# A six-mixer network on one core: the first loads in another order, two weight tiles split singly, half of x turned between products

## What is computed

```python
def short_conv_mixer(xn, w_in, conv_w, conv_b, w_out):
    bg, cg, hv, z = jnp.split(xn @ w_in, 4, axis=-1)
    u = cg * hv
    y = lax.conv_general_dilated(
        u, conv_w[:, None, :].astype(u.dtype), window_strides=(1,),
        padding=[(CONV_WIDTH - 1, 0)], dimension_numbers=("NWC", "WIO", "NWC"),
        feature_group_count=A_WIDTH) + conv_b
    return (bg * y * jax.nn.silu(z)) @ w_out
...
            y = short_conv_mixer(rmsnorm(x, a_norm[j]), a_w_in[j], a_conv_w[j], a_conv_b[j], a_w_out[j])
...
        x = x + y
```

## Time and profile before

| | us |
|---|---|
| timed runs | 931.11, 932.44, 932.61; median 932.44 |
| span of the profiled execution, first to last instruction | 928.8 |
| TensorE busy in it | 905.7 |
| VectorE, ScalarE, GpSimd busy | 649.8, 499.6, 299.3 |

### The profile page before, as it was taken

The page is one execution under the profiler, slowest core; times in us unless marked ns, Lnnn a source line. Parts: engine busy times, 40 slices in busy tenths (PEclk is TensorE's granted clock), DMA queues, the critical chain, the costliest instruction groups (busy, mean ns, idle before and its releaser), DMA issues.

```text
span 928.8 us, 16916 instructions
## 1 busy us (share of the span) xinstructions
PE 905.7 (98%) x6817; PEld 853.2 (92%) x6817; DVE 649.8 (70%) x1024; ACT 499.6 (54%) x732; POOL 299.3 (32%) x243
## 2 busy tenths in 40 slices
PE   8999999999989999989999999999999999999996
PEld 8999997788879987779999999999999998989996
DVE  5786666889785789865876676897735745656643
ACT  5644445664875669865444453343536336585632
POOL 8433322473111332113433218976003000223310
PEclk9999999999999999999999999999999999999998
DMA  9886436344414443445785535544664552525411
GB/s 247 234 224 181 181 106 240 121 140 169 147 60 150 143 134 112 145 117 153 183 225 187 182 137 182 178 146 178 236 217 164 209 182 91 181 92 181 165 41 46
DMA packets 123587, 148.72 MB, mean 160 GB/s; under 512 B 9562, under 2 KB 79103, under 8 KB 123519
## 3 DMA queue, kind: packets, MB, share of 16 engines
q1 hardware_dynamic: 121472, 145.63, 48.6%
q0 software_dynamic: 464, 1.02, 0.4%
q10 hardware_dynamic: 1582, 1.12, 0.4%
HBM read 146.70 MB, written 1.05 MB: 159 GB/s over the span
## 4 chain that ended last, share of the span: by engine, by line
PE 66%; DVE 9%; ACT 4%; POOL 1%; issue 1%; ACTq 0%; POOLq 0%; DVEq 0%
PE acc L1772 48%; PE aux L1772 17%; DVE wlo L931 2%; DVE wlo L952 1%; ACT work L705 1%; POOL sqy L1686 1%; ACT work L707 1%; DVE work L1270 1%; ACT work L720 1%; PE aux L2144 1%; DVE arena L1039 0%; DVE sqy L1130 0%; DVE hf L1140 0%; ACT arena L748 0%; ACT whi L491 0%
## 5 line engine op out<-in xcount | busy, mean ns | idle before, releaser
L931 DVE TENSOR_TENSOR wlo<-raw,whi 128x2048 fp32r<-128x2048 f32 (+5 forms) x114 | 273.5, 2421 | 81.7 <-ACT whi L483 79.7
L1772 PE MATMUL acc<-xh,whi 128*128 128x256 f32 x1128 | 321.7, 285 | 1.1 <-ACT arena L748 0.6
L1772 PE MATMUL acc<-xh,wlo 128*128 128x256 f32 x1128 | 319.1, 283 | 0.0
L1772 PE MATMUL acc<-xl,whi 128*128 128x256 f32 x1128 | 319.1, 283 | 0.0
L483 ACT ACTIVATE whi<-raw 128x2048 fp32r<-128x2048 f32 (+5 forms) x115 | 197.9, 1745 | 88.5 <-PE acc L1772 51.4
L1772 PEld LDWEIGHTS acc<-xh,whi 128*128 128x128 f32 x1128 | 215.9, 191 | 3.0 <-issue 1.6
L1772 PEld LDWEIGHTS acc<-xl,whi 128*128 128x128 f32 x1128 | 216.0, 191 | 0.0
L1772 PEld LDWEIGHTS acc<-xh,wlo 128*128 128x128 f32 x1128 | 215.9, 191 | 0.0
L1772 PE MATMUL aux<-yh,whi 128*128 128x256 f32 x288 | 82.3, 286 | 2.0 <-DVE stat L1274 2.0
L1772 PE MATMUL acc<-whi,xh 128*128 128x512 f32 (+1 forms) x208 | 81.4, 391 | 1.6 <-DVE arena L1039 0.5
L1772 PE MATMUL aux<-yl,whi 128*128 128x256 f32 x288 | 81.5, 283 | 0.0
(11 more groups left out here) (348 smaller groups left out, 1726.7 us busy)
## 6 DMA issues: line engine op xcount, KB each, us to landing
raw<-in_a_w_in SPq DMA_DIRECT2D x52, 512.0 KB, 6.7
raw<-in_sb_w_in SPq DMA_DIRECT2D x48, 512.0 KB, 5.5
raw<-in_b_w_in SPq DMA_DIRECT2D x36, 512.0 KB, 5.4
raw<-in_pool_w_in SPq DMA_DIRECT2D x32, 512.0 KB, 5.4
raw<-in_a_w_out SPq DMA_DIRECT2D x16, 512.0 KB, 4.9
raw<-in_pool_w_out SPq DMA_DIRECT2D x16, 512.0 KB, 5.7
raw<-in_sb_w_out SPq DMA_DIRECT2D x16, 512.0 KB, 5.2
raw<-in_b_w_out SPq DMA_DIRECT2D x8, 512.0 KB, 5.0
```

Of the source, the lines that this page charges most:

```text
L931: TT(wlo[b][:, lo:hi], (raw_third if third else raw[b])[:, lo:hi], whi[b][:, lo:hi].bitcast(F32), ALU.subtract).then_inc(lo_ready, 1)
L1772: return nc.tensor.matmul(out_, lhsT, rhs, start=start, stop=stop, skip_group_check=True)
```

## The change

The four issues of x on SP are taken apart: x's first half goes ahead of everything, the identity and the gain `a_norm` (from ScalarE's list) follow, then x's second half and the 48 rotary constants. The ten small rows move from ScalarE's list to SP's, behind the weight tiles of unit 0 and ahead of the other constants and unit 1's tiles. ScalarE's first instructions are now the two weight tiles, which get a semaphore each, and a load of its function table. GpSimd's four gain rows and mask move from ahead of the angles to behind them. Weight tiles 0 and 1 are split singly (`first_tile`), the other three quarters as before. TensorE does 14 and 5 idle products in place of 22 and 6, turns the first half of x, and turns the second half ahead of `k` 2 of unit 0 (`turn_x(1)`). VectorE and ScalarE have lists to match.

```diff
+            x_half(0)
+            sp.dma_start(ident, a["constants"][:, C_ID:C_ID + P]).then_inc(sem("ident_in"), 16)
+            sp.wait_ge(sem("grow_clear"), 1)
+            for dst, part in small_inputs(True):
+                sp.dma_start(dst, part).then_inc(sem("a_norm_in"), 16)
+            x_half(1)
+            sp.dma_start(cst[:, C_IROW:C_COLS], a["constants"][:, C_IROW:C_COLS]).then_inc(sem("inv_in"), 16)
...
                     for k in range(2, 8):
                         first_tile(0, k).then_inc(sem(f"first_in{k // 2}"), 16)
+                    for dst, part in small_inputs(False):
+                        sp.dma_start(dst, part).then_inc(sem("grow_in"), 16)
                     sp.dma_start(cst[:, P:C_IROW], a["constants"][:, P:C_IROW]).then_inc(sem("cst_in"), 16)
...
-                    .then_inc(sem("first_in0"), 16)
-            small_inputs(False)
+                    .then_inc(sem(f"tile_in{k}"), 16)
+            nc.scalar.preload_act_table_set("exp_and_others")
+
+            def first_tile(k):
+
+                c = slice(512 * k, 512 * k + 512)
+                act.wait_ge(sem(f"tile_in{k}"), 16)
+                A(whi[0][:, c], raw[0][:, c], ACT.Copy).then_inc(sem("first_hi") if k else sem("tile_hi"), 1)
...
                     for n in range(NK):
+                        if m == 0 and n in (0, 2):
+                            first_tile(n // 2)
+                        if m == 0 and n in (4, 5, 7):
+                            first_quarter(0, n - 3 if n < 7 else 3)
                         act.wait_ge(sem("x_ready"), 4 * m + n // 2 + 1)
                         A(xh[:, n, :], xT[:, n, :], ACT.Copy, scale=G[:, gain + n:gain + n + 1])\
                             .then_inc(sem("xh_ready"), 1)
-                        if m == 0 and n % 2:
-                            first_quarter(0, n // 2)
...
+                turned(0)
+                first_tile(0)
+                turned(1)
+                low(0)
+                first_tile(1)
+                low(1)
+                first_quarter(0, 1)
+                turned(2)
+                turned(3)
+                first_quarter(0, 2)
+                low(2)
+                low(3)
+                first_quarter(0, 3)
...
-                    if u < 2 and k % 4 == 0:
+                    if u == 0 and k == 0:
+                        pe.wait_ge(sem("tile_lo"), 1)
+                    if u < 2 and k % 4 == (1 if u == 0 and k < 4 else 0):
                         pe.wait_ge(sem("first_lo"), 2 * u + k // 4 + 1)
...
                 def before(k):
+                    if k == 2 and m == 0:
+                        turn_x(1)
                     pe.wait_ge(sem("xl_ready"), 8 * m + k + 1)
...
-            busy(22)
+            busy(14)
...
+            turn_x(0)
+            busy(5)
```

More of the change, by code:

```diff
@@ L335, in free_slot, with small_inputs @@
             eng.wait_ge(lo_ready, 2 * u - 2)
+        def small_inputs(first):
+            rows = ((G_A, "a_norm", 16), (G_CW, "a_conv_w", 48), (G_CB, "a_conv_b", 16), (G_B, "b_norm", 8),
+                    (G_C, "c_norm", 8), (G_N2, "norm_g_2", 16),
+                    (G_QL, "c_q_lat_norm", 3), (G_KVL, "c_kv_lat_norm", 2))
+            found = [(grow[col:col + c, 0, :], a[name].rearrange("(n c) -> n c", c=P))
+                     for col, name, c in (rows[:1] if first else rows[1:])]
+            if first:
+                return found
+            return found + [(grow[G_CQ:G_CQ + 1, 0, 0:64], a["c_q_norm"][:, 0:64]),
+                            (grow[0:1, 1, 0:64], a["c_k_norm"][:, 0:64]),
+                            (grow[1:17, 1, :], a["pool_scale_2"].rearrange("(n c) -> n c", c=P))]
         @block.sync
@@ L400, in conv_layer, with x_half @@
                     plain(u0 + 8 + h, a["a_w_out"][j], 4 * h, 0)
-            sp.dma_start(ident, a["constants"][:, C_ID:C_ID + P]).then_inc(sem("ident_in"), 16)
-            sp.dma_start(cst[:, C_IROW:C_COLS], a["constants"][:, C_IROW:C_COLS]).then_inc(sem("inv_in"), 16)
-            for half in range(2):
+            def x_half(half):
                 c = slice(512 * half, 512 * half + 512)
@@ L966, in split, with first_tile, first_x, turned @@
                     split_half(u % 2, cut, end)
+            def first_tile(k):
+                c = slice(512 * k, 512 * k + 512)
+                dve.wait_ge(sem("first_hi") if k else sem("tile_hi"), 1)
+                TT(wlo[0][:, c], raw[0][:, c], whi[0][:, c].bitcast(F32), ALU.subtract)\
+                    .then_inc(sem("first_lo") if k else sem("tile_lo"), 1)
+            def first_x():
+                def turned(c):
+                    dve.wait_ge(sem("x_psum"), c + 1)
+                    V.tensor_copy(xT[:, 2 * c:2 * c + 2, :], aux[:, c, :].rearrange("p (n t) -> p n t", n=2))\
+                        .then_inc(sem("x_ready"), 1)
+                def low(c):
+                    dve.wait_ge(sem("x_ready"), c + 1)
+                    for n in (2 * c, 2 * c + 1):
+                        dve.wait_ge(sem("xh_ready"), n + 1)
+                        STT(xl[:, n, :], xT[:, n, :], G[:, G_A + n:G_A + n + 1], xh[:, n, :].bitcast(F32),
+                            ALU.mult, ALU.subtract).then_inc(sem("xl_ready"), 1)
+                turned(0)
[11 more added lines that the diff above has]
+                first_quarter(0, 3)
             def renorm(m, gain):
@@ L1640, in by_token @@
                 return ap.rearrange("p (t c) -> p t c", t=1).broadcast_to([P, NT, ap.shape[1]])
+            for n, name in enumerate(("b_q_norm", "b_k_norm")):
+                pool.dma_start(gain_b[:, n, :], a[name].broadcast_to([P, 64])).then_inc(sem("gain_in"), 16)
+            for n, name in enumerate(("c_q_norm", "c_k_norm")):
+                pool.dma_start(gain_c[:, n, :], a[name][:, 64:96].broadcast_to([P, 32])).then_inc(sem("gain_in"), 16)
+            pool.dma_start(mask[:, :], a["chunk_mask"]).then_inc(sem("mask_in"), 16)
             pool.wait_ge(sem("gain_in"), 64)
@@ L1875, in _, with turn_x @@
             pe.wait_ge(sem("warm_ready"), 1)
-            busy(22)
+            busy(14)
             pe.wait_ge(sem("ident_in"), 16)
[L1878 to L1890, removed]
+            def turn_x(half):
+                pe.wait_ge(sem(f"x_in{half}"), 32)
+                for n in range(4 * half, 4 * half + 4):
+                    for t in range(NT):
+                        ins = nc.tensor.transpose(aux_tile(n)[:, t * P:t * P + P], xrow[:, t, n * P:n * P + P], ident)
+                    if n % 2:
+                        ins.then_inc(sem("x_psum"), 1)
+                    if n == 1:
+                        pe.wait_ge(sem("a_norm_in"), 16)
+                        nc.tensor.transpose(acc[:, 3, 0:16], grow[0:16, 0, :], ident[0:16, 0:16])\
+                            .then_inc(sem("ga_psum"), 1)
+            turn_x(0)
+            busy(5)
             def transpose_parameters():
```

36 lines of the change are left out of this document (4 added, 32 removed).

## The result

| | before | after |
|---|---|---|
| median of the timed runs | 932.33 us (17 runs, 931.11 to 933.39) | 934.50 us (17 runs, 933.30 to 936.02) |
| ratio, 95% interval | | 1.0025 [1.0018, 1.0032] |
| profiled execution: span | 928.8 us | 932.9 us (own time 934.74) |

The change makes the kernel 2.2 us slower (1.7 to 3.0), where 0.2 us of gain was forecast. An execution's own time is 1.8 above its span in the changed kernel, and 1.6 to 1.7 in later runs of the kernel before. By that the profiled execution of before took an estimated 930.4, 1.9 under its median, so the two spans lie further apart (4.1) than the medians (2.2). I therefore compare dates within the first 130 us.

A forecast was written before the change was run, and what follows sets the result against it. TensorE was taken to bound the kernel, its start paid in full. A 3.2 us head start less 1.1 (turns), 1.0 and 0.7 (waits) and 0.25 (border) left 0.2: 932.44 - 0.2 = 932.2 us, range 930.4 to 934.2.

The forecast's parts named there:

- First part: Start of unit 0: x's first half goes out earlier, first product at 10.1 instead of 13.32, a head start of 3.2.
- Second part: Inside unit 0: turns take back 1.1, two waits 1.0 and 0.7, the border 0.25; 0.2 us is left.
- rival A: Start: tiles 2 and 3 land by 10.6, no wait ahead of the turns, head start stays; 930.7, chance 0.22.
- Z: Moment in unit 0 when TensorE's wait for the low part of tiles 2 and 3 ends; put at 14.0.
- Third part, weights: Behind unit 0: ten small issues on SP take 3.3, `raw_third` is whole at 33.3; costed at nothing.
- rival B: Ahead of unit 2: ten small loads cost SP 5 us, `raw_third` comes at 35, TensorE waits 1.7; 934.0, chance 0.11.
- D: Unit 2: GpSimd's tables late by a microsecond, 933.5, chance 0.07; near 934.5 if descriptor writing delays the rows 2.5.
- C: TensorE's start: rests lower the clock, `k` 0 and 1 take 5.8 for 2.9, 1.9 lost; 934.1, chance 0.06.
- Third part, GpSimd: Unit 2: angles some 2 later, `upad` ends near 39.1, second half ready at 43.2, wanted at 43.3; just covered.

The follow-up runs named there:

- f1: Changed kernel with the 48 rotary constants issued by SP between the first norm's gains and x's second half; ratio to before 1.0024.
- e6: Kernel before with only the gain rows and the mask moved behind the angles; ratio to before 0.9999.
- e7: Kernel before with only the 48 rotary constants issued behind x's second half; ratio to before 1.0031.
- g4: g1 with the norm's root put ahead of the sines on ScalarE; ratio to before 0.9990.
- g1: Changed kernel with the four gain rows and the mask issued by ScalarE near 11 us, constants still late; ratio to before 1.0015.
- f2: f1 with the four gain rows and the mask issued by ScalarE behind the second quarter of unit 0; ratio to before 0.9992.
- e1: Changed kernel with GpSimd's four gain rows and the mask issued ahead of the angles again; ratio to before 1.0021.
- e2: Changed kernel with the 48 rotary constants issued by ScalarE behind its two weight tiles; ratio to before 1.0028.

## Why the prediction was wrong

**First part, right.** First turn 6.96 (6.6 forecast), first product 10.45 (10.1), a head start of 2.9 for 3.2.

**Second part, one of its two waits did not come.** Tiles 2 and 3 were there at 10.88, when ScalarE took them, not at 11.6. So the turns stood at 13.39 with no wait ahead of them (1.0 forecast), which is the sign written down for rival A, and Z is 13.4, between the forecast's 14.0 and rival A's 13.0. `k` 4 came 4.86 behind Z with a wait of 0.95 (4.7 and 0.7). TensorE was 0.86 ahead behind unit 0, not 0.2; the earlier Z is nearly all of the difference. Up to here the change was better than forecast.

**Third part, weights: right.** The ten issues took 3.95 for 3.3; unit 1's first issue stood at 14.26, `raw_third` was taken at 32.39 (33.3 forecast). TensorE waits for none of them. The sign written down for rival B did come, a wait of over 0.5 on the low part of `raw_third` (1.49), but B's cause did not: ScalarE had that half rounded at 37.8, and VectorE stood idle for `upad` until 41.76, which is D's sign. The granted clock read 1.00 and the products stayed 0.12 apart behind each rest, so not C either.

**Third part, GpSimd: this is the step that failed**, "Its angles wait for constants behind x's second half, some 2 later", to "Just covered". Two things are wrong in it.

The size: the angles start 2.5 later (9.21 for 6.72), near the forecast's 2, but end 5.5 later (29.3 for 23.8), because the same 24 operations take 20.1 instead of 17.1. The forecast had moved the list without asking whether it would keep its length. In before:

```profile
6.72 0.18 POOL L1609 CAST pos_f<-pos_i 128x2 f32<-128x2 int32 x1 [1.56 <-DMA pos_i<-in_positions]
...
17.91 1.06 POOL L1621 TENSOR_TENSOR work<-ang 128x96 f32<-128x96 f32 x1
...
23.18 0.59 POOL L1625 TENSOR_SCALAR work<-work 128x96 f32<-128x96 f32 x1
```

In the changed kernel:

```profile
15.70 0.45 POOL L1654 TENSOR_SCALAR ang<-ang 128x96 f32<-128x96 f32 x1
...
22.82 1.45 POOL L1655 TENSOR_TENSOR work<-ang 128x96 f32<-128x96 f32 x1
24.36 1.30 POOL L1654 TENSOR_SCALAR ang<-ang 128x96 f32<-128x96 f32 x1
```

beside VectorE's

```profile
22.81 5.09 DVE L952 TENSOR_TENSOR wlo<-raw,whi 128x1024 fp32r<-128x1024 f32 x4
```

The same operation takes 0.45 with VectorE idle and 1.30 within unit 1's four low parts. The Trainium skill ("SBUF — State Buffer", Who interferes with whom) says that a VectorE instruction with two inputs in SBUF contends with a GpSimd instruction that reads SBUF; the two durations agree. Of the 24 operations eight take 1 us or more, in before five, and each of these runs for at least 0.8 beside a `TENSOR_TENSOR` of VectorE, a low part of weights or a sum of squares.

Four of the eight fall into unit 1's low parts, but the delay is not made there: as these begin, GpSimd is already 4.9 behind (22.82 for the same operation at 17.91), and only 0.6 are added until the end. Nor is the later start enough to explain it: in f1 the list starts at 7.62 and takes 20.9, and in e6, where VectorE keeps the list of before, it starts at 7.95 and takes 18.5. So the length hangs on what VectorE does beside each operation, and the change had reordered VectorE's list too. How the 3.0 us divide between the later start and the new order is not shown.

I had drawn on that page of the Trainium skill for loads alone, in rival D. These rows do not test that: they were issued in 0.53 to 0.63 each, four of the five while VectorE rested (28.3 to 31.4). The gain rows landed 5.1 to 5.7 later, like the load of 5.8.

From there all dates of the step are 3 late: rows issued at 29.25 (26), landed at 36.6 (33.7), `upad` done at 41.7 (39.1), the second half ready at 45.9 (43.2). Rival D had the place and the sign, at "a microsecond more"; it was three. D's other figure, 934.5, is the measured median by luck: it came from loads that land late behind their issue, and these did not. The second half's date alone sets the lag: TensorE takes it at 45.99, where before took it at 43.54.

The omission: the angles have a second reader. ScalarE's sines stand ahead of the norm's root, so TensorE's spread hangs on GpSimd too. I read the earlier trace rows for GpSimd's wait on the sines, and not who waited behind the sines. In before ScalarE was ready for the sines at 28.1, 4.3 behind the angles; in the changed kernel it was ready at 27.5 and the angles came at 29.3. e7 shows that path alone, g4 that turning the order round removes it. In the changed kernel the later date in unit 2 covers it; with that one gone it decides (g1, a lag of 1.1).

What each is worth: in the kernel before, the gain rows' late place alone costs nothing (e6), and the constants alone cost 0.31% (e7, where they land 3.2 later than in the change). In the changed kernel, constants put earlier alone give 0.01% back (f1), the gain rows on ScalarE alone 0.10% (g1), both 0.33% (f2).

## What to carry to other kernels

Follow a transfer that is moved back to every reader of what it starts, on every engine, and ask what the other engines, whose lists changed too, will do beside the late list: 2.5 us at its start became 5.5 at its end. When two rests follow each other, undo both before judging either, since the later date hides the earlier one. And look for an idle issuer in a thin stretch of the stream before choosing between first and last: in the changed kernel the same five loads cost the front when first (e1), unit 2 when last, and nothing that shows in between (f2, g4).

## What was not expected of the hardware

An earlier issue was no earlier landing: the 24 KB of constants, issued by ScalarE at 2.12 behind two 256 KB tiles, landed at 8.9 (e2, GpSimd started at 9.02); issued by SP at 2.88, behind 584 KB of x, identity and gain, they landed at 7.5 (f1, 7.62). Why SP's were through sooner was not traced. Five loads of 288 KB in all, issued by GpSimd from 2.50 on in e1, moved the landing of SP's identity block from 6.9 to 9.3; in the other kernels with the new front the first turn stood between 6.75 and 7.59. And the clock: behind a rest of 2.50 us, before the first turn of e1, TensorE's granted clock went from 1.00 to 0.50 for a stretch (the lower of the two levels, 1.2 of 2.4 GHz); behind a rest of 3.27 us in e7, which followed 20 us of products, it stayed at 1.00. What told the two apart was not tried.
